# Two attention heads per step handled together: scores, softmax and value matmuls of both heads interleaved

## What is computed

```
for l in range(DEPTH):                       # DEPTH = 2
    shift, scale, gate = jnp.split(cond @ w_ada[l] + b_ada[l], 3, axis=-1)
    proj = (x * (1.0 + scale[:, None]) + shift[:, None]) @ w_in[l]
    y_a = a_b * causal_dwconv(a_c * a_x, conv_a[l]) * silu(a_g)
    y_b = dilated_attention(q * HD ** -0.5, k, v, rel_bias) * silu(b_g)   # 8 heads of 64
    y_c = rglru_branch(c_x, ...) * silu(c_g)
    y_d = s5_branch(d_u, ...) * silu(d_g)
    y = jnp.concatenate([y_a, y_b, y_c, y_d], axis=-1) @ w_out[l]
    x = layer_norm(ALPHA * x + (1.0 + gate[:, None]) * y, ln_g[l], ln_b[l])
```

## Time and profile before

| | us |
|---|---|
| median of 3 runs | 2034.84 (2034.25 to 2038.93) |
| the profiled execution | 2038.36, its span 2036.6 |
| PE busy with matmuls | 1800.5 (88%) |
| DVE busy | 1203.3 (59%) |
| ACT busy | 805.3 (40%) |
| projection matmuls of the branch loop, L867, L868, L874 | 3 x 1536 |
| scores L792, passes | 128 |
| value matmuls L809, passes | 128 |
| waits of L792 for DVE | 17.8 in 7 waits, the longest 4.0 |

### The profile page before, as it was taken

One profiled execution on the slowest core, in us unless ns is written; L12 is line 12 of the kernel. 1 busy time (PEld: TensorE's weight loads), 2 busy tenths in 40 slices (PEclk: granted clock), 3 DMA queues, 4 the chain that ended last, 5 costly groups with the idle time before them and its releaser, 6 DMA issues.

```text
span 2036.6 us, 22811 instructions
## 1 busy us (share of the span) xinstructions
PE 1800.5 (88%) x7335; PEld 1325.6 (65%) x7335; DVE 1203.3 (59%) x2333; ACT 805.3 (40%) x1042; POOL 276.3 (14%) x341
## 2 busy tenths in 40 slices
PE   1329999999999999898896999999999999979993
PEld 0217667767766866656775767866776776647783
DVE  5685874784586488443445486387468458540625
ACT  1004443534434443432332544444454454443331
POOL 2122111101111111101112311111111111101110
PEclk9558999999999999999998999999999999989997
DMA  6989679867967986839996867976886787729883
GB/s 216 331 287 247 165 186 221 217 157 197 233 162 195 229 205 158 210 107 285 267 274 190 196 161 170 216 177 159 199 188 164 180 200 170 175 70 303 219 194 124
DMA packets 331585, 407.53 MB, mean 200 GB/s; under 512 B 28024, under 2 KB 224992, under 8 KB 328424
## 3 DMA queue, kind: packets, MB, share of 16 engines
q1 hardware_dynamic: 294632, 272.36, 41.2%
q0 software_dynamic: 36864, 134.23, 35.7%
HBM read 261.81 MB, written 10.51 MB: 134 GB/s over the span
## 4 chain that ended last, share of the span: by engine, by line
PE 62%; DVE 21%; DMA 10%; issue 3%; ACT 2%; SPq 1%; POOL 0%; DVEq 0%; ACTq 0%
PE bank L867 14%; PE bank L868 13%; PE bank L874 13%; DVE work L1165 7%; DMA w_lo<-raw 6%; DVE ada_acc L1173 4%; PE bank L920 4%; PE bank L911 3%; PE bank L912 3%; DMA raw<-in_w_out 2%; PE bank L792 2%; PE bank L809 2%; PE bank L766 2%; PE bank L886 2%; DVE y_t L1173 2%
## 5 line engine op out<-in xcount | busy, mean ns | idle before, releaser
L867 PE MATMUL bank<-op_hi,w_hi 128*128 128x512 f32 x1536 | 625.7, 407 | 0.5 <-ACT w_hi L545 0.5
L868 PE MATMUL bank<-op_lo,w_hi 128*128 128x512 f32 x1536 | 608.2, 396 | 0.0
L545 ACT ACTIVATE w_hi<-raw 128x1024 fp32r<-128x1024 f32 x256 | 271.3, 1060 | 700.9 <-PE bank L868 476.9
L496 POOL DMA_DIRECT2D w_lo<-raw x256 | 222.3, 868 | 1561.5 <-ACT w_lo L548 1522.3
L874 PE MATMUL bank<-op_hi,w_lo 128*128 128x512 f32 x1536 | 379.7, 389 | 2.4 <-DMA w_lo<-raw 2.3
L867 PEld LDWEIGHTS bank<-op_hi,w_hi 128*128 128x128 f32 x1536 | 294.0, 191 | 113.0 <-issue 53.0
L868 PEld LDWEIGHTS bank<-op_lo,w_hi 128*128 128x128 f32 x1536 | 294.1, 191 | 60.9 <-issue 1.9
L548 ACT ACTIVATE w_lo<-raw 128x1024 fp32r<-128x1024 f32 x256 | 270.5, 1057 | 157.9 <-PE bank L874 124.0
L874 PEld LDWEIGHTS bank<-op_hi,w_lo 128*128 128x128 f32 x1536 | 288.1, 188 | 63.2 <-DMA w_lo<-raw 3.5
L1173 DVE SCALAR_TENSOR_TENSOR ada_acc<-ada_in,cond,ada_acc 128x512 f32<-128x512 f32 (+1 forms) x241 | 189.6, 787 | 199.3 <-DMA ada_in<-in_w_ada 183.9
L911 PE MATMUL bank<-w_hi,op_hi 128*128 128x512 f32 x512 | 200.4, 391 | 0.7 <-ACT w_hi L545 0.7
(11 more groups left out here) (195 smaller groups left out, 1582.5 us busy)
## 6 DMA issues: line engine op xcount, KB each, us to landing
w_lo<-raw POOLq DMA_DIRECT2D x256, 512.0 KB, 5.0
raw<-in_w_in SPq DMA_DIRECT2D x192, 512.0 KB, 3.9
ada_in<-in_w_ada SPq DMA_DIRECT2D x256, 256.0 KB, 4.4
raw<-in_w_out SPq DMA_DIRECT2D x64, 512.0 KB, 5.7
raw<-in_w_ada SPq DMA_DIRECT2D x24, 512.0 KB, 5.2
ada_in<-in_w_ada SPq DMA_DIRECT2D x16, 512.0 KB, 5.7
bias_t<-in_w_ada SPq DMA_DIRECT2D x8, 512.0 KB, 5.2
work<-in_w_ada SPq DMA_DIRECT2D x8, 512.0 KB, 6.4
```

Source lines behind the costliest of these rows:

```text
L496: pool.dma_start(w_lo[:, n % NHL, :], raw[:, n % NRAW, :], accum_op=ALU.add)\
L545: act.activation(w_hi[:, n % NHL, :], raw[:, n % NRAW, :], ACT.Copy).then_inc(s.hi_done.sem, 1)
L867: pe.matmul(o, w_hi[:, n % NHL, w], op_hi[:, k, :], start=k == 0, stop=False)
L868: mm = pe.matmul(o, w_hi[:, n % NHL, w], op_lo[:, k, :], start=False, stop=False)
```

## The change

Both heads go through attention together. The scores of query tile t of head 0 go to bank 5 and those of head 1 to bank 6, each cut into two halves, in the order head 0, head 1, head 0, head 1; they stand at n = 9, 10, 12 and 13. Head 0 uses rows 0 to 63 of the array and head 1 rows 64 to 127. There is one round of exps (eight activations at ACT's n = 14), one normalise, and three turns (key block 0; blocks 1 and 3 in one bank; block 2) at n = 16, 18 and 20, with their copies in ACT's list at n = 18, 20 and 22 and the value matmuls at n = 18, 20 and 22, in which the heads alternate and write the two halves of bank 7's partitions. Blocks 1 and 3 are cut into halves. Head 1's probabilities lie in ada_acc, prob and v_t, its transposed ones in q_t and k_t; gel moves to s5_s[3]. DVE's s5_tile is cut into s5_in, s5_scan and s5_out, and one score_max(t) for both heads stands before or between these parts; the ada pieces are as many as before, in other places. Counts of the semaphores follow (they are left out below, and so are the buffers' names).

```
...
-                    def exps(h):
-                        act.wait_ge(s.to_act.sem, s.to_act.at(2 + h, ct))
-                        for t in range(ST):
...
+                    def exps():
+                        act.wait_ge(s.to_act.sem, s.to_act.at(2, ct))
+                        for h in range(2):
+                            for t in range(ST):
+                                i = ST * h + t
+                                e = act.activation(prob_of[h][t], prob_of[h][t], ACT.Exp, bias=soft[:, 1, i:i + 1],
+                                                   scale=1.0, accum_out=soft[:, 2, i:i + 1])
                         e.then_inc(s.from_act.sem, 1)
...
+                    def p_copy(g):
+                        n = sum(P * (ST - kb) for kb in TURNS[g])
+                        if g != 1:
+                            act.wait_ge(s.pv_done.sem, s.pv_done.at(g, ct))
+                        for h in range(2):
+                            act.wait_ge(s.full[5 + h].sem, s.full[5 + h].at(1 + ST + g + 1, ct))
+                            act.activation(p_t[h][g % 2][:, 0:n], bank[5 + h][:, 0:n], ACT.Copy).then_inc(s.p_copy.sem, 1)
...
                         if n == 13:
-                            exps(0)
                             gate("c_g", 0, 0)
                         if n == 14:
...
                             act.activation(work[:, 10, :], bank[7][:, :], ACT.Copy).then_inc(s.free[7].sem, 1)
+                            exps()
                         if n == 15:
                             gate("d_g", 1, 0)
-                        if n == 16:
-                            p_copy(0, 0)
-                            p_copy(0, 1)
+                        if n in (18, 20, 22):
+                            p_copy((n - 18) // 2)
...
+                    def scores(t):
...
+                        n = P * (t + 1)
+                        for h in range(2):
+                            is_free(5 + h, 1 + t)
+                        for w in (slice(0, n // 2), slice(n // 2, n)):
+                            for h in range(2):
+                                heads = slice(64 * h, 64 * h + 64)
+                                mm = pe.matmul(bank[5 + h][:, w], q_t[heads, P * t:P * (t + 1)], k_t[heads, w],
+                                               start=True, stop=True)
+                                if w.start:
+                                    fill(5 + h, mm)
...
+                    def weigh(g):
+                        pe.wait_ge(s.p_copy.sem, s.p_copy.at(2 * g + 2, ct))
+                        if g == 0:
                             is_free(7, 1)
...
+                        for kb in TURNS[g]:
+                            n = P * (ST - kb)
+                            for w in (slice(0, n // 2), slice(n // 2, n)) if kb % 2 else (slice(0, n),):
+                                for h in range(2):
+                                    mm = pe.matmul(bank[7][64 * h:64 * h + 64, P * kb + w.start:P * kb + w.stop],
+                                                   v_s[:, kb, 64 * h:64 * h + 64],
+                                                   p_t[h][g % 2][:, TURN_AT[kb] + w.start:TURN_AT[kb] + w.stop],
+                                                   start=kb == 0, stop=kb == 2)
+                                    if w.stop == n:
+                                        mm.then_inc(s.pv_done.sem, 1)
...
-                    for h, at in ((0, 10), (1, 17)):
-                        for t in range(ST):
-                            put(at + t // 2, scores, h, t)
+                    for t, at in enumerate((9, 10, 12, 13)):
+                        put(at, scores, t)
                     put(11, v_turn)
...
+                    for g, (at_turn, at_weigh) in enumerate(((16, 18), (18, 20), (20, 22))):
+                        put(at_weigh, weigh, g)
+                        put(at_turn, p_turn, g)
                     put(HALF - 1, ada_sum)
...
-                s5_tile(1, 2, 1)
-                score_max(0, (0, 1))
-                ada(2, 1)
-                score_max(0, (2, 3))
-                ada(2, 1)
-                normalise(0)
-                s5_tile(2, 2, 1)
+                score_max(0)
+                s5_in(1)
+                s5_scan(1)
+                ada(2, 1)
+                score_max(1)
+                s5_out(1)
+                ada(2, 1)
+                score_max(2)
+                s5_in(2)
+                ada(2, 1)
+                score_max(3)
+                s5_scan(2)
+                ada(2, 1)
+                s5_out(2)
+                normalise()
+                ada(2, 1)
                 own(silu2(0, "c_g", gx[:, 0, :]), s.own)
...
-                ada(2, 1)
-                s5_tile(3, 2, 1)
-                score_max(1, (0, 1))
-                ada(2, 1)
-                score_max(1, (2, 3))
+                s5_in(3)
+                s5_scan(3)
+                ada(2, 1)
+                s5_out(3)
                 own(silu2(1, "d_g", silu_d[:, bass.ds(ct, 1), :].rearrange("p o t -> p (o t)")), s.gate_used[1])
                 ada(2, 1)
-                normalise(1)
...
+                ada(2, 1)
                 own(silu2(0, "b_g", gx[:, 0, :]), s.own)
```

More of the change, by code:

```diff
@@ L178, in trunk @@
         lru_s = [work[:, 11 + i, :] for i in range(3)]
[L179 removed]
+        p_t = [(work[:, 14, :], work[:, 15, :]), (q_t, k_t)]
         gx = work[:, 16:18, :]
@@ L782, in lru_gates @@
                             fill(5 + i, pe.matmul(bank[5 + i][:, :], lru_w[:, i, :], xc, start=True, stop=True))
-                    def scores(h, t):
-                        b = 5 + t % 2
-                        if h == 0 and t == 0:
+                    def scores(t):
+                        if t == 0:
                             unit_copied(pe, s, "q", ct)
                             unit_copied(pe, s, "k", ct)
-                        if h == 1:
-                            pe.wait_ge(s.p_copy.sem, s.p_copy.at(ST, ct))
-                        is_free(b, 1 + 2 * h + t // 2)
-                        fill(b, pe.matmul(bank[b][:, 0:P * (t + 1)], q_t[64 * h:64 * h + 64, P * t:P * (t + 1)],
-                                          k_t[64 * h:64 * h + 64, 0:P * (t + 1)], start=True, stop=True))
@@ L805, in weigh @@
-                    def weigh(h, kb):
-                        pe.wait_ge(s.p_copy.sem, s.p_copy.at(4 * h + kb + 1, ct))
-                        if h == 0 and kb == 0:
-                            is_free(7, 1)
-                        pe.matmul(bank[7][64 * h:64 * h + 64, P * kb:S], v_s[:, kb, 64 * h:64 * h + 64],
-                                  p_t[:, kb % 2, 0:P * (ST - kb)], start=kb == 0, stop=kb == ST - 1)\
-                            .then_inc(s.pv_done.sem, 1)
+                        n = P * (t + 1)
@@ new lines, in p_turn @@
+                    def p_turn(g):
+                        if g == 0:
+                            pe.wait_ge(s.p_norm.sem, s.p_norm.at(1, ct))
+                        for h in range(2):
+                            if g:
+                                pe.wait_ge(s.p_copy.sem, s.p_copy.at(2 * (g - 1) + h + 1, ct))
+                            for kb in TURNS[g]:
+                                for t in range(kb, ST):
+                                    at = TURN_AT[kb] + P * (t - kb)
+                                    mm = pe.transpose(bank[5 + h][:, at:at + P], prob_of[h][t][:, P * kb:P * (kb + 1)],
+                                                      ident[:, :])
+                            fill(5 + h, mm)
@@ L1057, in s5_tile, with score_max @@
                     own(tt(x_im, x_im, t_, ADD), s.x_rot)
-                def score_max(h, ts_):
-                    for t in ts_:
-                        b, use = 5 + t % 2, 1 + 4 * h + t // 2
-                        w = P * (t + 1)
-                        dve.wait_ge(s.full[b].sem, s.full[b].at(use + 1, ct))
-                        dve.wait_ge(s.mix_in.sem, s.mix_in.at(96, ct))
+                def score_max(t):
+                    for h in range(2):
+                        b, i, w = 5 + h, ST * h + t, P * (t + 1)
+                        dve.wait_ge(s.full[b].sem, s.full[b].at(1 + t + 1, ct))
+                        if t == 0 and h == 0:
+                            dve.wait_ge(s.mix_in.sem, s.mix_in.at(96, ct))
+                        if t == ST - 1 and h == 1:
+                            dve.wait_ge(s.full[7].sem, s.full[7].at(1, ct))
@@ L1066, in score_max @@
                         line(dve.memset(spare[:, :], 0.0), s.own)
-                        own(dve.tensor_tensor_reduce(prob[:, P_AT[t]:P_AT[t] + w], bank[b][:, 0:w],
-                                                      bias_t[:, h, S - w:S], 1.0, -3e38, ADD, ALU.max,
-                                                      soft[:, 0, t:t + 1]), s.free[b])
-                    if ts_[-1] == 3:
+                        own(dve.tensor_tensor_reduce(prob_of[h][t], bank[b][:, 0:w], bias_t[:, h, S - w:S], 1.0, -3e38,
```

(19 more changed lines are left out.)

81 lines of the change are left out of this document (27 added, 54 removed).

## The result

| | before | changed |
|---|---|---|
| time, median of 4 runs (lowest to highest), us | 2036.86 (2034.25 to 2038.93) | 2000.59 (1999.22 to 2004.38) |
| ratio to before, 95% interval | | 0.9827 [0.9809, 0.9846] |
| profiled execution, us (its span) | 2038.36 (2036.6) | 2004.38 (2002.6) |

The change makes the kernel 1.7% faster. Timed once more beside later experiments, the same kernel took 1995.78 us, 0.9812 [0.9799, 0.9825] of the kernel before.

The account below looks back on a forecast made before the run. PE was taken to bound the kernel, with its waits for DVE. Terms -27.5 - 1.9 + 32 - 19 - 6.1 - 4.8 = -27.3 gave 2007.5 us against the median of 2034.84; range 1995 to 2044.

Parts of the forecast that it names:

- old stall: PE's score wait for DVE goes: -27.5 us in layer 0 with its slow clock, -1.9 in layer 1.
- new stall at block 15: Exps ahead of block 15's weights in ACT's queue make PE wait 1.9 and 2.1 us a step, +32 over eight.
- clock behind the gate-vector sum, layer 0: With less thin work around layer 0's gate-vector sum the clock stays up: 3 steps x 1.6, -4.8 us.
- Part 1: PE's own work: about 0 a step if serial; partial overlap of the two heads saves 2.4 us a step, -19.
- rival 5: Scores and values: a pair of both heads' matmuls costs one duration, half of 8.5 us a step; 1992.5 us, chance 0.07.
- Part 2: Cutting DVE's S5 tiles removes PE's score wait in each step; later drive and output covers are thin, without a wait.
- rival 4: DVE misses the thin margins of Part 2 by 2 us a step, +16 or more: 2024 to 2035; chance 0.06.
- Part 3: Block 15's w_hi and w_lo come late behind ACT's exps: two waits, 4.0 us a step, +32; clock stays up.
- Rival 2: Clock takes block 15's two waits for one, +2.9 x 8 = +23: 2030.5 with overlap, chance 0.09; 2050 without, 0.03.
- Part 4: Layer ends: values finish at n=22, w_glu load 3.05 us sooner per layer, -6.1; clock after layer 0's gate-vector sum, -4.8.
- 1 (nothing overlaps): Scores and values: the two heads' passes don't overlap, the forecast without the 19; 2026.5 us, chance 0.19.
- 3 (a switch between heads costs): Scores and values: each head change costs PE up to 0.2 us, +34, 2060; 2043 at 0.1; chance 0.14.

Follow-up runs that it names:

- e4: Kernel before, with only head 0's score_max for tiles 0 and 1 moved from behind the S5 tile into it; 2006.4 us, ratio 0.9850.
- c_after: The changed kernel, unaltered, timed and profiled once more beside later experiments; 1995.8 us, ratio 0.9812 to the kernel before.
- e14: Changed kernel with score matmuls cut into quarters, all eight passes of head 0 issued before the eight of head 1; 2024.4 us, ratio 0.9951.
- e1: Changed kernel with halves kept but heads not alternating: all passes of head 0, then all of head 1; 2009.3 us, ratio 0.9859.
- e3: Changed kernel with the eight exps moved to n=15, behind the cast of block 15 and the d_g gate; 1964.7 us, ratio 0.9635.
- e8: Changed kernel with both heads' score matmuls reading the same rows, partitions 0 to 63; 2017.2 us, ratio 0.9909.
- e5: Changed kernel with the last value group put back to n=23, ahead of the gate-vector sum; 2004.5 us, ratio 0.9827.
- e6: Changed kernel with no matmul cut into halves, the heads alternating whole matmuls; 1996.5 us, ratio 0.9797.
- e13: e6 with four value passes of head 0 before four of head 1 in the middle value group; 1997.6 us, ratio 0.9819.
- e12: Changed kernel with head 1's value matmuls writing head 0's partitions, so both use the same columns; 2016.5 us, ratio 0.9891.
- e5b: Second run of e5, last value group at n=23, beside the unaltered changed kernel; 2001.3 us, ratio 0.9846.

## Why the prediction was right, and which terms were off

The span went from 2036.6 to 2002.6, so 34.0 us; the measured terms add up to 33. The terms, in the prediction's order:

| term | forecast | measured | from |
|---|---|---|---|
| old stall, layer 0 and layer 1 | -29.4 | -29.4 | waits of 17.8 gone; 4 x 2.9 of clock, as 174.07 - 167.12 = 6.95 in e4 shows |
| fall without a wait, layer 1 | not in it | -1.5 | 166.15 against 165.28 - 0.63 |
| new stall at block 15 | +32 | +28.6 | 8 x 1.73, and 1.81 to 1.88 |
| clock at block 15 | 0 | +6.4 | 4 falls x 1.6 |
| two heads at once | -19 | -34 | 8 x 4.3 |
| ends, up to the w_glu matmuls | -6.1 | -2.4 | 1.6 and 0.8 less from the last sum of a layer on |
| behind them | 0 | +4.1 | +1.0 in the profile of c_after; cause open |
| clock behind the gate-vector sum, layer 0 | -4.8 | -4.8 | 1.00 in three steps |
| sum | -27.3 | -33 | |

**Part 1** failed in its step "two passes of one head still follow each other (high, low), and the second head can start beside the first one's low pass": five pass times of eight. The trace shows two passes, one of each head, 6 ns apart, throughout. The prediction reasoned as if one pass at a time entered and only the tail overlapped. The floor of 0.11 us was right for one head's scores (e14: 0.11 from start to start at 32 and at 128 columns), but not for the pair: eight passes of 64 columns take 0.59 us, four pairs at 0.11 and the entry. The short value passes, with 64 columns of weights, have a lower floor: 0.058 us from start to start at 64 columns in e1's middle group. So rival 5, given 0.07, was the mechanism and the size of this term (8 x 4.25 = 34), and its objection was what was wrong. With -34 for -19 the forecast's sum would have been -42; the other terms took 8 of it back. The rule of the Trainium skill that stood beside this part ("TensorE: Matmul & The Clock Gate", Part 3: concurrent tiles, starts some 4 ns apart) agrees with the trace, at 6 ns.

**Part 2** was right: no wait at scores(2), none of the thin margins missed (rival 4). With the new stall in place the later ones are not tested; e3 takes that stall away and one of them shows, 0.6 to 0.7 us in four steps. What it overlooked is the one step of layer 1 before without the wait of 0.63, which had a fall of the clock in its place.

**Part 3** was right in its mechanism, its place and its times to 0.1 us, and 0.4 us a step too high in its sum: block 14 ended at T + 5.75 and not T + 5.45, so both waits were shorter than 1.9 and 2.1. Rival 2 was put as all or nothing, with 2.9 us a step. It came true in half of the steps at 1.6: the first, second and fourth step of layer 0 and the first of layer 1, the same four in both profiled runs of this kernel. The reason for the 0, "each is below 2.32", did not hold even for one wait: the clock fell after single waits of 2.39 and 2.24 us. Two of 1.73 and 1.87, with 3.6 us of work between, lower it or not. In the other kernels with both waits it fell at block 15 in none (e8), one (e14), two (e5), three (e6, e13), four (e12, e5b) or six (e1) of eight steps, and not always in the same ones. What tells the steps apart was not found.

**Part 4** was right about the layer's last block (3.58 us from its end to the load, 3.6 forecast) and about the clock. It was wrong in what that is worth. Of the 3.05 us, 0.8 is the value group, which PE now does before block 23: counted from the start of the last gate-vector sum, the load of w_glu stood at +5.93 and stands at +3.74, 2.2 us sooner, and 2.1 in layer 1. Then the transfer takes longer, 5.65 us instead of 5.04 and 6.60 instead of 5.28 in layer 1 (5.72 and 6.50 in c_after), so that PE starts on the w_glu matmuls 1.6 and 0.8 us sooner. What became of these 2.4 us can't be told. From there on the kernel takes 4.1 us more than before in this profile, outside the steps; in the profile of c_after it is 1.0. Why the transfers got slower was not tried. e5b, with its 2.1 us at the same two places, says that the part is not empty.

The rivals: 1 (nothing overlaps) and 3 (a switch between heads costs) fall with the pairs; whoever alternates 12 times pays nothing that the groups show. e1, with fewer changes of head, is not faster but slower. The forecast missed 15 us in the pairs, 3 in the new stall and 1.5 in layer 1, all to the fast side; on the other side it missed 6 in the clock, 4 in the ends and 4 behind them. These went against each other by luck. A time 7 us from the forecast hides errors larger than itself, and the result doesn't bear out the size that part 1 gave.

## What to carry to other kernels

Two fp32 matmuls that fill half of the array each cost one, provided that they take different rows (here with a bank each) or different columns (here in one bank, in other partitions), and that no more than some four passes of the one stand ahead of the other in the queue; halving or strict alternation is not needed for it. When work of two units is joined, look at the queue of the engine that feeds PE: here eight exps in one piece delayed one block's weights and gave back 35 of some 70 us that had been won, and moving them by one cast got it back. And a small version of one half of the change is worth a run of its own: the early score_max alone brought 31 us.

## What the runs showed of the hardware that was not expected

- PE's matmuls don't start strictly in program order: in e1's middle value group a pass of head 1 started before the sixth to eighth pass of head 0 that stand ahead of it. In both kernels with eight passes in turn the other head came in beside the fifth.
- Narrow fp32 passes over 64 rows start every 0.11 us whether they have 32, 64, 96 or 128 columns (1.55 to 1.71 us for sixteen in e14), and every 0.11 us two of them where they are in pairs.
- Two waits of less than 1.9 us, 3.6 us of work apart, lowered the granted clock to 0.64 over the next 4.7 us in four steps of eight, where a single wait of 2.32 had not. Single waits of 2.24 and 2.39 did lower it elsewhere, and one of 2.31 didn't.
- The granted clock fell to 0.50 while PE was busy without a break, behind 1.98 us of 32-row and 0.92 us of 64-row matmuls (the kernel before, 1530.44), and four times in e8, whose score groups are longer.
